# Compressed branch of a sparse attention: token copies inside the projection, keys block-diagonal per head pair, two passes on GpSimd

## The reference

```python
def compress(x, pe, w1, w2):
    B, T, G, d = x.shape
    chunks = x.reshape(B, T // CMP_STRIDE, CMP_STRIDE, G, d)
    blocks = jnp.concatenate([chunks[:, :-1], chunks[:, 1:]], axis=2) + pe[None, None, :, None, :]
    flat = blocks.transpose(0, 1, 3, 2, 4).reshape(B, -1, G, CMP_LEN * d)
    return jnp.einsum('bngf,fe->bnge', jax.nn.gelu(flat @ w1), w2)

k_cmp = compress(rope(kv(kc_raw), pos), pe[0], w1[0], w2[0])
v_cmp = compress(kv(vc_raw), pe[1], w1[1], w2[1])
...
s = jnp.einsum('bqghd,bngd->bqghn', qb, k_cmp).astype(jnp.float32) * scale
p_cmp = safe_softmax(s, (cmp_end[None, :] <= t[:, None])[:, None, None, :])
o_cmp = jnp.einsum('bqghn,bngd->bqghd', p_cmp.astype(v_cmp.dtype), v_cmp)
```

## Time and profile before

| | us |
|---|---|
| median of 3 runs | 3455.22 |
| lowest, highest | 3454.71, 3459.01 |
| span of the profiled execution | 3463.4 |
| TensorE busy | 3252.7 (94%) |
| VectorE busy | 1826.3 (53%) |
| GpSimd busy | 1334.0 (39%) |
| ScalarE busy | 1303.2 (38%) |
| mean granted TensorE clock | 0.956 |

### The profile page before, as it was taken

One profiled execution on the slowest core, in us unless ns is written; L12 is line 12 of the kernel. 1 busy time (PEld: TensorE's weight loads), 2 busy tenths in 40 slices (PEclk: granted clock), 3 DMA queues, 4 the chain that ended last, 5 costly groups with the idle time before them and its releaser, 6 DMA issues. The chain is left out here.

```text
span 3463.4 us, 48142 instructions
## 1 busy us (share of the span) xinstructions
PE 3252.7 (94%) x16380; PEld 2680.7 (77%) x16380; DVE 1826.3 (53%) x3756; ACT 1303.2 (38%) x2179; POOL 1334.0 (39%) x830
## 2 busy tenths in 40 slices
PE   7999999898889999999999987899999988999999
PEld 6867787798888888888888854478888864478887
DVE  7404324887748777777777377432212336642211
ACT  4234433245543333333334334333322215633322
POOL 2323352288862222222221323434444316734443
PEclk9889999999999999999999998799999988999999
DMA  5321242244569999999997310023323420023332
GB/s 121 81 70 32 73 109 75 60 153 172 197 240 341 323 325 317 332 317 325 322 321 242 82 49 25 9 83 97 97 85 99 118 55 1 1 86 97 97 90 80
DMA packets 453881, 502.00 MB, mean 145 GB/s; under 512 B 77409, under 2 KB 398241, under 8 KB 435825
## 3 DMA queue, kind: packets, MB, share of 16 engines
q1 hardware_dynamic: 430448, 363.77, 34.3%
q0 software_dynamic: 18432, 134.23, 10.5%
q10 hardware_dynamic: 4864, 2.23, 0.3%
HBM read 458.06 MB, written 38.80 MB: 143 GB/s over the span
## 5 line engine op out<-in xcount | busy, mean ns | idle before, releaser
L125 POOL TENSOR_TENSOR w_low<-w_ring,w_high 128x1024 fp32r<-128x1024 f32 (+3 forms) x317 | 758.2, 2395 | 1136.4 <-ACT w_high L120 1108.8
L136 PE MATMUL ps<-h_low,w_high 128*128 128x512 f32 (+1 forms) x2432 | 918.5, 378 | 54.1 <-POOL w_low L125 28.3
L137 PE MATMUL ps<-h_high,w_high 128*128 128x512 f32 (+1 forms) x2432 | 900.6, 370 | 0.0
L138 PE MATMUL ps<-h_high,w_low 128*128 128x512 f32 (+1 forms) x2432 | 900.5, 370 | 0.0
L136 PEld LDWEIGHTS ps<-h_low,w_high 128*128 128x128 f32 x2432 | 464.0, 191 | 125.9 <-POOL w_low L125 31.8
L137 PEld LDWEIGHTS ps<-h_high,w_high 128*128 128x128 f32 x2432 | 463.9, 191 | 63.8 <-issue 6.3
L138 PEld LDWEIGHTS ps<-h_high,w_low 128*128 128x128 f32 x2432 | 462.9, 190 | 56.9
L120 ACT ACTIVATE w_high<-w_ring 128x1024 fp32r<-128x1024 f32 (+3 forms) x317 | 323.9, 1026 | 123.6 <-PE ps L138 120.0
L136 PE MATMUL ps<-v_low,top 128*128 128x512 f32 x768 | 299.7, 390 | 6.6 <-DVE v_low L125 6.6
L138 PE MATMUL ps<-v_high,top_at 128*128 128x512 f32 x768 | 300.8, 392 | 0.0
L137 PE MATMUL ps<-v_high,top 128*128 128x512 f32 x768 | 300.7, 392 | 0.0
(11 more groups left out here) (538 smaller groups left out, 5452.7 us busy)
## 6 DMA issues: line engine op xcount, KB each, us to landing
w_ring<-in_peer_uv_dram SPq DMA_DIRECT2D x128, 512.0 KB
u_raw<-in_peer_uT_dram SPq DMA_DIRECT2D x78, 512.0 KB, 6.0
w_ring<-in_peer_uT_dram SPq DMA_DIRECT2D x50, 512.0 KB, 3.8
gates<-peer_gates SPq DMA_DIRECT2D x31, 768.0 KB, 11.4
w_ring<-in_ffn_w_gate_dram SPq DMA_DIRECT2D x44, 512.0 KB, 3.7
w_ring<-in_ffn_w_up_dram SPq DMA_DIRECT2D x44, 512.0 KB, 3.7
w_ring<-in_w_in_dram SPq DMA_DIRECT2D x36, 512.0 KB, 3.8
w_ring<-in_ffn_w_down_dram SPq DMA_DIRECT2D x32, 448.0 KB, 3.8
```

The lines of the kernel that those rows point to most:

```text
L125: return eng.tensor_tensor(rounded(low), whole, high, ALU.subtract)
L136: nc.tensor.matmul(out, rounded(w_high), rounded(x_low), start=start, stop=False, **more)
L137: nc.tensor.matmul(out, rounded(w_high), rounded(x_high), start=False, stop=False, **more)
L138: return nc.tensor.matmul(out, rounded(w_low), rounded(x_high), start=False, stop=stop, **more)
```

## The change

- The key copies are issued by SyncE inside the projection, once ten tiles are made and behind SyncE's weight loads. They go into `key_tokens`, the first five tiles of the output buffer `oT`, which is not in use yet. GpSimd clears its fifth group in the projection too. The value copies are issued in the branch, two by SyncE, two by ScalarE ahead of its other work.
- The position terms are copied for keys and values apart, each with its own count.
- TensorE makes the keys as soon as the keys' hidden part is there, and the values' second product moves behind the scores.
- The compressed keys of a group pair are laid out block-diagonally (`kc_pairs`, zeros elsewhere), so that a score matmul takes two heads at a time: 128 rows, 64 moving columns, 8 in a token tile instead of 16, all into one bank.
- Subtraction of the maximum and weighing go from VectorE to GpSimd. VectorE alternates: maximum of tile t, share of tile t-1. Second mask and guard for empty rows stay for token tile 0 alone.
- After the transposes of each token tile TensorE runs four warm-up matmuls.

```diff
+        if "sp_made" in after:
+            after["sp_made"](sp, lambda tiles: sp.wait_ge(bank_free, per_turn + tiles))
...
+        def copy_tokens(eng, tokens, source, z, b):
+            for after in range(2):
+                eng.dma_start(tokens[half(after), 2 * b:2 * b + 2, 0:T - after], source[half(b), 0:2, after:T]).then_inc(tokens_in[z], 16)
+        def copy_keys(sp, wait_made):
+            wait_made(KEYS_MADE)
+            for b in range(2):
+                copy_tokens(sp, key_tokens, kT, 0, b)
+        def pad_keys(pool):
+            nc.gpsimd.memset(key_tokens[:, 4, :], 0.0).then_inc(keys_padded, 1)
+        projections(load, vcT, {"sp_made": copy_keys, "pool": pad_keys})
...
             @block.sync
             def _(sp):
-                for z in range(2):
-                    for b in range(2):
-                        for after in range(2):
-                            sp.dma_start(tokens[half(after), z, 2 * b:2 * b + 2, 0:T - after], source[z][half(b), 0:2, after:T]).then_inc(tokens_in[z], 16)
+                copy_tokens(sp, value_tokens, vcT, 1, 0)
...
+                def less_top(t):
+                    pool.wait_ge(topped, t + 1)
+                    nc.gpsimd.tensor_tensor(s[:, t, :, :], s[:, t, :, :], stat[:, 0, t, :].unsqueeze(2).to_broadcast(full), ALU.subtract).then_inc(less, 1)
+                def weigh(t):
+                    pool.wait_ge(shared, t + 1)
+                    nc.gpsimd.tensor_tensor(s[:, t, :, :], s[:, t, :, :], stat[:, 1, t, :].unsqueeze(2).to_broadcast(full), ALU.mult).then_inc(weighed, 1)
+                less_top(0)
+                for t in range(1, TT):
+                    less_top(t)
+                    weigh(t - 1)
+                weigh(TT - 1)
...
-                pe.wait_ge(hid, 4)
+                pe.wait_ge(hid, 2)
                 for b in range(2):
                     mm = nc.tensor.matmul(c.ps[half(b), 0, 0:2 * NP], w2[:, 0, :], hidden[:, 0, b, :, :].rearrange("p i n -> p (i n)"), start=True, stop=True)
-                mm.then_inc(kv_made, 1)
+                mm.then_inc(k_made, 1)
+                pe.wait_ge(k_done, 2)
+                for t in range(TT):
+                    for pair in range(NSA_H // 2):
+                        mm = nc.tensor.matmul(c.ps[:, score_bank[t], pair * 2 * NP:(pair + 1) * 2 * NP], qT[:, pair, t * P:(t + 1) * P],
+                                              kc_pairs[:, pair // NSA_HPG, :, :].rearrange("p b n -> p (b n)"), start=True, stop=True)
+                    mm.then_inc(scored, 1)
...
-                for t in range(TT):
-                    for h in range(NSA_H):
-
-                        i, j, b = h // 8, (h // 2) % 4, h % 2
-                        mm = nc.tensor.matmul(c.ps[:, 2 * t + b, (h // 2) * NP:(h // 2 + 1) * NP], qT[half(b), 4 * i + j, t * P:(t + 1) * P], kcT[half(b), i, :],
-                                              start=True, stop=True)
-                    mm.then_inc(scored, 1)
...
                     tr.then_inc(turned, 1)
+                    spin(c, score_bank[1], 4)
             @block.scalar
             def _(act):
...
+                copy_tokens(act, value_tokens, vcT, 1, 1)
...
-                nc.scalar.activation(kcT[:, :, :], c.ps[:, 0, 0:2 * NP].rearrange("p (i n) -> p i n", i=2), ACT.Copy).then_inc(kv_done, 1)
...
+                for b in range(2):
+                    nc.scalar.activation(kc_pairs[half(b), :, b, :], c.ps[half(b), 0, 0:2 * NP].rearrange("p (i n) -> p i n", i=2), ACT.Copy).then_inc(k_done, 1)
...
+                top_of(0)
                 dve.wait_ge(hid, 4)
                 for a in range(2):
                     v.tensor_copy(spread[:, :, a, :, :], hidden[:, 1, :, :, :].rearrange("p b i n -> p i b n")).then_inc(spread_done, 1)
...
+                for t in range(1, TT):
+                    top_of(t)
+                    share_of(t - 1)
+                share_of(TT - 1)
```

More of the change, by code:

```diff
@@ L3723, in odd_mix, with projections @@
             vcr = mixing.sbuf("vcr", [P, 2, NSA_D])
-            def projections(load, vcT):
+            def projections(load, vcT, after):
                 with c.stage() as inner:
@@ L3733, in projections @@
                     project_rope(c, w["qkv"], [rope.of[64]] * 4, lambda i, b: NSA_D ** -0.5 if i < 2 else 1.0, lambda i, b: dests[4 * i + b], w["out"],
-                                 {"sp": load, "dve": lambda dve: reorder_gates(c, dve, gates, order)}, unturned=len(dests) - 2)
-            compressed(c, A, w, qT, kT, order, pcT, vcr, projections)
+                                 {"sp": load, "dve": lambda dve: reorder_gates(c, dve, gates, order)}, after, unturned=len(dests) - 2)
+            compressed(c, A, w, qT, kT, order, pcT, vcr, oT[:, 0:5, :], projections)
             nsa_attention(c, qT, kT, vs, vw, order, pcT, vcr, oT)
@@ L3749, in reorder_gates, with compressed @@
     step.wait()
[L3752 removed]
+def compressed(c, A, w, qT, kT, order, pcT, vcr, key_tokens, projections):
     nc = c.nc
@@ L3762, in compressed @@
         masks = ctx.sbuf("masks", [P, 2, TT, NP])
-        cmp_in = ctx.sem("cmp_in")
+        cmp_in, keys_padded = ctx.sem("cmp_in"), ctx.sem("keys_padded")
+        tokens_in = [ctx.sem(f"tokens_in{z}") for z in range(2)]
+        half = lambda b: slice(64 * b, 64 * b + 64)
         def load(sp):
@@ L3781, in compressed @@
         spread = ctx.sbuf("spread", [P, 2, 2, 2, NP])
-        kcT = ctx.sbuf("kcT", [P, 2, NP])
+        kc_pairs = ctx.sbuf("kc_pairs", [P, 2, 2, NP])
         s = ctx.sbuf("s", [P, TT, NSA_H, NP])
         stat = ctx.sbuf("stat", [P, 2, TT, NSA_H])
[L3785 to L3790, removed]
+        padded, made, biased, hid, spread_done, k_made, k_done, v_made, v_done, pe_turned, pe_moved = (
+            ctx.sem(n) for n in ("padded", "made", "biased", "hid", "spread_done", "k_made", "k_done", "v_made", "v_done", "pe_turned", "pe_moved"))
+        scored, topped, less, exped, shared, weighed, turned, copied = (
+            ctx.sem(n) for n in ("scored", "topped", "less", "exped", "shared", "weighed", "turned", "copied"))
+        made_bank, score_bank, turn_bank = (4, 6), (2, 3, 5, 7), (4, 6, 0, 2)
+        full = [P, NSA_H, NP]
         with nc.Block() as block:
@@ L3846, in _ @@
-                act.wait_ge(padded, 1)
-                nc.scalar.activation(tokens[:, :, 4, 0:2 * PAIRS_L:2], c.ps[:, 1, 0:2 * PAIRS_L].rearrange("p (z m) -> p z m", z=2), ACT.Copy).then_inc(pe_moved, 1)
+                copy_tokens(act, value_tokens, vcT, 1, 1)
+                for z in range(2):
+                    if z == 0:
+                        act.wait_ge(pe_turned, 1)
+                        act.wait_ge(keys_padded, 1)
+                    else:
+                        act.wait_ge(padded, 1)
+                    nc.scalar.activation(tokens[z][:, 4, 0:2 * PAIRS_L:2], c.ps[:, 1, z * PAIRS_L:(z + 1) * PAIRS_L], ACT.Copy).then_inc(pe_moved, 1)
```

72 lines of the change are left out of this document (35 added, 37 removed).

## The result

| | before | after |
|---|---|---|
| median of 5 runs, us | 3457.03 | 3440.58 |
| lowest, highest | 3454.71, 3459.01 | 3434.76, 3448.90 |
| span of the profiled execution | 3463.4 | 3446.6 |

The account below looks back on a forecast made before the run. TensorE is busy nearly throughout, so a change pays only where it waits or works slowly. Gains of 5.3 + 1.0 + 6.8 + 1.8 = 14.9 us from the 3455.2 median give 3440.3 us; eight in ten, 3434.5 to 3446.

Parts of the forecast that it names:

- Key copies inside the projection: Key copies issued behind SyncE's weight loads hold nobody and land at about 2807, 8 us before they are needed.
- Product start: Compression product starts at 2815.5, 5.3 us earlier (4.6 to 5.9), after ScalarE's two value-copy issues and position copy.
- Product unchanged: The compression product keeps its 17.2 us.
- Hand-over: From product end to first score 1.2 us instead of 2.2, so 1.0 us less (0.8 to 1.2).
- The block-diagonal form gives nothing at equal clock: Scores: 64 full-height records cost about what 128 half-height ones do, 13.9 us at 1.2 GHz, 7.5 at 2.4.
- The clock in the scores: Scores were forecast wholly at the low clock, 13.9 us; the full clock was kept as a rival.
- First score to warm-ups: Scores and softmax to the end of the turns: 22.5 us instead of 29.3, 6.8 less; barrier 0.9 unchanged.
- Rival 1: Clock stays full through scores and turns, which end at 20.0 us; gain 17.4, time 3437.8 us; chance 0.20.
- Warm-ups behind the turns: New warm-ups raise the clock, so the attention's own eight warm-ups take half of 3.57 us, 1.8 less.
- rival 4: GpSimd's eight broadcast passes become the bound in the softmax; 3465.4 us at 5 us a pass; chance 0.02.
- rival 3: Key copies land late or ScalarE's issues hold the product; 5.3 us lost, 9.6 gained, 3445.6 us; chance 0.03.
- rival 5: Something unseen, such as the attention's clock or a moved buffer, gives the gain back; about 3452 us; chance 0.05.

Follow-up runs that it names:

- fill_sync: Changed kernel plus four warm-up matmuls behind the key product, with all four value copies on SyncE; ratio 0.9942, stage 41.78 us.
- row_halves: Changed kernel with the old score form, one half-height matmul per head, 128 records; ratio 0.995, scores 11.40 us.
- no_warm: Changed kernel without the four warm-up matmuls behind each turn; ratio 0.9957, scores 11.41 us, stage 46.38 us.
- pause: Changed kernel with ten ScalarE copies ahead of the two key copies, so that TensorE pauses 7.76 us; ratio 0.9973, scores 13.50 us.
- vector_passes: Changed kernel with subtraction and weighing back on VectorE, in the new alternating order; ratio 0.995, first score to warm-ups 22.19 us.
- before_order: Old kernel with only VectorE's alternating order (maximum of a tile, share of the tile before); ratio 1.0, first score to warm-ups 27.48 us.
- after_again: The changed kernel run a second time, nothing edited; 3437.28 us, ratio 0.9938, stage 44.87 us.
- before_warm: Old kernel with seven warm-up matmuls between product and scores, nothing else; ratio 0.999, stage 61.17 us.

## Why the prediction was right, step by step

- **Key copies inside the projection: right.** They are issued 11.5 us ahead of the stage, and the product doesn't wait for them.
- **Product start: mechanism right, a term too small.** Forecast 5.3 us, measured 4.85. ScalarE's two issues, put at 1.3 between 0.8 and 2.0, took 1.73; fill_sync shows them to be the bound.
- **Product unchanged: right**, 17.2 us in all kernels.
- **Hand-over: right**, 1.0 forecast, 1.1 measured.
- **The block-diagonal form gives nothing at equal clock: right**, shown by row_halves beside no_warm. The forecast durations of 64 records, 13.9 and 7.5 us, came out at 13.5 and 7.08. The Trainium skill, page "TensorEngine Tiling (Array Packing)", section "Performance Considerations", advises 2x row tiling for a contraction of 64. The trace agrees in cost: two overlapped halves take as long as one full record. What moved the time of the scores here was the clock.
- **The clock in the scores: wrong as a forecast, and half as a rival.** All-low scores came only with a pause of 7.8 us; with 1.2 the clock was lost 2.2 to 2.6 us into the scores in four of five executions of the full-height form, and kept in the one profiled with the result. The forecast took the old pause's behaviour for the new one's. Between the two executions of the same kernel that is 4.5 us of scores, of which 2.4 reach the warm-up matmuls.
- **First score to warm-ups: both cases came out too long.** The forecast was 22.5 and 0.9 of barrier, 23.4; the same case, in pause, took 21.9. Rival 1 was 20.0 and 0.9, 20.9; it took 17.9. In the first case the step at fault is the moment at which the clock rises in the turns: put at 19.3 us behind the first score, measured at 16.8. So one turn of 2.48 us ran at the low clock and not two of 2.56, and the turns ended at 21.1 instead of 22.5; the barrier is most of what is left. In the second case it is sizes. GpSimd's pass was put at 1.28 us and took 1.05. VectorE's small product was to wait up to 1.3 us and took 0.24 instead of 0.17. The copy of the values' hidden part was put at 1.5, blocked, and its two pieces took 0.35 together. The last weighing ended 15.6 us behind the first score instead of 18.2 (2854.45 in after): 1.15 of these 2.6 are the copy, the rest lies in the shares and in GpSimd's passes. Blocking as such exists, but by more than 0.1 us only where VectorE reads two inputs from SBUF over full width: the second mask (1.60 or 1.59 in place of 1.05 or 0.69). The Trainium skill, page "SBUF — State Buffer", section "Who interferes with whom", says that a VectorE instruction with two inputs in SBUF and a GpSimd instruction that reads SBUF contend for a shared port, on which one blocks the other. The trace agrees for that mask; the first mask, which reads PSUM, and the sums kept their 0.69 beside GpSimd's passes.
- **Warm-ups behind the turns: right**, 1.8 forecast, 1.7 measured against no_warm.
- **What the prediction did not separate**: the GpSimd passes are worth 1.9 us (vector_passes), the alternating order alone 2.7 in the old kernel (before_order). Together with the 2.4 of the clock these are 7.0 of the 12.3 us between first score and warm-ups, read in different kernels, so they need not add up. Second mask and guard for one tile only, and the copies moved beside the turns, were not run apart; the cause of the other 5.3 is open. In before, second mask and guard took 1.14 us of VectorE's time in each tile (0.72 from 2858.75 to 2859.47, 0.42 from 2860.19 to 2860.61), which for the three tiles left out makes an estimate of at most 3.4.
- **Slower by GpSimd (rival 4), nothing gained by the copies (rival 3), something that gives it back (rival 5)**: none came. The passes are far under 3.7 us. The time behind the stage was 588 to 592 us in all the kernels, 589.5 in before.

The sum of the stage was 14.9 us, the profiled execution gave 19.8 and the second one 17.4. The whole time gave 16.5 between medians, and its interval reaches from 12.1 to 22.5 us (0.35% and 0.65% of 3457.03), so it would have agreed with any of the three. The hit on the number is therefore luck in good part: a wide target, and a median that moves too (the six runs of after_again have theirs at 3437.28). The direction and the order of the terms were right; the size was 2.5 to 5 us low, and that lies between first score and warm-ups.

## What to carry to other kernels

Where the gain is half a per cent, cut the changed stage at its own events and compare that; the work ahead of it moved by as much as the change is worth. Price a denser matmul form twice: at equal clock, where two overlapping halves may already cost what one full record does, and by the clock that the form and the pause ahead of it leave. Issue copies of data that is ready early behind earlier loads, on a queue whose engine has nothing else due: here the product started 6.35 us earlier than before with all later issues on SyncE, and 4.85 with two of them on ScalarE.

## What the runs showed of the hardware

- Scores right behind a filled pause: the full-height records kept 1.00 over 7.08 us in three executions, the half-height ones fell to a mean of 0.83 over 8.43 us in the one that was run, and to 0.61 over 11.24 us in the old kernel (before_warm, its pause busy for 2.36 of 2.73 us). Why is open; both kept TensorE busy in the whole stretch, and with one execution each of the half-height form it may also be chance.
- Behind a pause of 1.15 us the same kernel once kept the clock and once lost it (1.00 and 0.59 over the scores), with the same instructions ahead of it in the stage. What decides was not found; with the pause filled it was kept over the scores in the three executions seen, and lost behind them.
- When GpSimd's pass and VectorE's two-input pass over 128x512 start together, either may be the one that is stretched: 1.60 and 0.69 us in four executions, 1.05 and 1.59 in one. In the second case the rest was 0.9 us longer.
- GpSimd's two-input pass with a broadcast operand took 1.05 us, less than the 1.28 of the earlier trace rows.
